# Seven products of sums of blocks for eight in the three last FFN stages of a float32 decoder trunk

## The chip, the core and the metric

The kernel runs on one core of a Trainium2 chip. The metric is the time on the device in microseconds, the median of several runs. TensorE is PE in the rows (its weight loads are PEld), VectorE is DVE, ScalarE is ACT, GpSimd is POOL, SyncE is SP. "us" is a microsecond.

## The reference

Two layers, each with two half-step SwiGLU FFNs around a mixer. The change is in the FFNs.

```python
D_MODEL = 1024; SEQ = 256; DEPTH = 2; D_FF = 2816
def _swiglu_ffn(h, w_in, w_out):
    gu = h @ w_in                      # (256, 1024) @ (1024, 5632)
    gate, up = jnp.split(gu, 2, axis=-1)
    return (jax.nn.silu(gate) * up) @ w_out

for i in range(DEPTH):
    x = x + 0.5 * _swiglu_ffn(_rmsnorm(x, ffn_norm[i, 0]), ffn_w_in[i, 0], ffn_w_out[i, 0])
    x = x + mixer(_rmsnorm(x, mix_norm[i]))     # layer 0: conv module, layer 1: differential attention
    x = x + 0.5 * _swiglu_ffn(_rmsnorm(x, ffn_norm[i, 1]), ffn_w_in[i, 1], ffn_w_out[i, 1])
```

## The kernel before

Six stages run one after the other: FFN, conv, FFN, FFN, attention, FFN, numbered 0 to 5. All weights come from HBM once, in units of 128 x 2048 float32 (1 MB), through three slots `raw`. Every matrix product is made of three in the round format fp32r: a weight `w` is split in `w_hi`, its rounding, and `w_lo`, the remainder, and so is the other side (`a_hi` and `a_lo` for the turned input of a stage, `h_hi` and `h_lo` for the turned hidden values). The product is the sum of hi x hi, hi x lo and lo x hi in PSUM (lines 563, 567 and 571). ACT does the roundings (`round_half`, line 985, 1024 columns each), DVE the remainders (`rest_half`, line 1397). Rounded forms stand in a ring of six places; ACT may overwrite a place once PE has begun the unit after the one that used it (`unit_begun`).

An FFN's 2816 hidden values go in 11 chunks of 256. A chunk has three units: two with its gate and up columns (one for each half of the 1024 inputs; `first_unit`, 24 matmuls of 512 columns each, over 4 blocks of inputs and 2 tiles of 128 tokens), and one with its rows of `w_out` (`second_unit`, 24 matmuls into `acc`, which holds the stage's sum in four banks). After the first two, ACT takes silu of the gate (line 1030) and DVE multiplies with up (`gated`, line 1489). The hidden values are turned by 16 DVE transposes of 32 partitions (`turn_hidden`, line 1497), rounded by ACT (`hidden`, line 1035), and DVE makes their remainder (line 1504). The second unit of a chunk stands one chunk later in PE's order, so all this has the time of the next chunk's first units. In PSUM a chunk takes the two banks of `pg`; the two of `pt` are for transposes.

The order on each engine is written by hand: `tick(n)` is the rounding or the remainder of unit n + 4, and the ticks stand between the steps of the chunks. At a stage's start (`enter`) DVE adds `acc` to `xs` (line 1413), multiplies with the norm's gain (1420), PE turns (667), ACT rounds (998), and squares are summed (1009).

## Time and profile before

| | |
|---|---|
| time, median of 3 runs | 951.86 us (951.72 to 951.97) |
| span of the profiled run | 950.0 us |
| PE busy, matmuls | 943.8 us, 4392 matmuls |
| DVE busy | 762.9 us |
| ACT busy | 495.2 us |
| from one FFN stage to the next (2 to 3) | 182.1 us |

The profile is one execution. Busy times of an engine are summed without overlap over its instructions; the mean of one matmul is longer than the distance to the next, since matmuls overlap. A releaser is what ended an engine's idle time.

### The profile page before, as it was taken

How to read it: one execution, taken by the hardware profiler on the slowest of the kernel's cores; microseconds unless marked ns; L12 is line 12 of the kernel's file. 1: busy time of each engine (PE TensorE's matmuls, PEld its weight loads, DVE VectorE, ACT ScalarE, POOL GpSimd, SP SyncE). 2: the span in 40 equal slices, each digit the busy share in tenths (PEclk: the TensorE clock that was granted, in tenths of full speed). 3: DMA queues.
4: the chain of work that ended last, by engine and by line, in shares of the span. 5: the costliest groups of instructions: out<-in, count | busy, mean ns of one | idle time of the engine just before them, and what ended most of it. 6: DMA issues, size and time to landing. Idle time of an engine off the chain costs nothing.

```text
span 950.0 us, 12305 instructions
## 1 busy us (share of the span) xinstructions
PE 943.8 (99%) x4392; PEld 778.6 (82%) x4392; DVE 762.9 (80%) x1447; ACT 495.2 (52%) x777; POOL 102.3 (11%) x94
## 2 busy tenths in 40 slices
PE   9999999999999999999999999999999999999998
PEld 7888888888978888888888888888778888888887
DVE  5778887879989887878788787877777888878782
ACT  6644353468755454444555344445778745444440
POOL 0100000068802000000000000001333100000000
PEclk9999999999999999999999999999999999999999
DMA  9876555544547636364554636353434545364521
GB/s 326 334 284 238 205 181 216 209 176 148 185 165 248 229 139 259 132 241 157 222 184 163 251 132 254 145 226 134 172 117 150 179 177 219 135 240 158 225 84 45
DMA packets 29548, 182.47 MB, mean 192 GB/s; under 512 B 3520, under 2 KB 3904, under 8 KB 9408
## 3 DMA queue, kind: packets, MB, share of 16 engines
q1 hardware_dynamic: 27360, 175.19, 48.9%
q0 software_dynamic: 2144, 6.70, 2.3%
q8 instruction: 26, 0.43, 0.2%
q14 instruction: 18, 0.15, 0.0%
HBM read 180.83 MB, written 1.05 MB: 191 GB/s over the span
## 4 chain that ended last, share of the span: by engine, by line
PE 98%; DMA 0%; DVE 0%; POOL 0%; ACT 0%; issue 0%; SPq 0%
PE pg L563 17%; PE pg L571 17%; PE pg L567 17%; PE acc L563 13%; PE acc L571 13%; PE acc L567 13%; PE pt L786 2%; PE pt L667 1%; PE acc L893 1%; PE pt L912 1%; DMA raw<-in_units 0%; PE acc L615 0%; PE pt L874 0%; PE acc L620 0%; PE acc L623 0%; PE pt L697 0%
## 5 line engine op out<-in xcount | busy, mean ns | idle before, releaser
L1397 DVE TENSOR_TENSOR w_lo<-raw,w_hi 128x1024 fp32r<-128x1024 f32 x304 | 356.4, 1221 | 18.2 <-ACT w_hi L985 16.9
L985 ACT CAST w_hi<-raw 128x1024 fp32r<-128x1024 f32 x314 | 311.2, 1046 | 20.7 <-DMA raw<-in_units 20.6
L563 PE MATMUL pg<-w_hi,a_hi 128*128 128x512 f32 x720 | 282.6, 392 | 0.0
L571 PE MATMUL pg<-w_hi,a_lo 128*128 128x512 f32 x720 | 280.3, 389 | 0.0
L567 PE MATMUL pg<-w_lo,a_hi 128*128 128x512 f32 x720 | 280.2, 389 | 0.0
L1497 DVE STREAM_TRANSPOSE mix<-hs 32x128 f32<-32x128 f32 x592 | 179.2, 303 | 8.9
L563 PEld LDWEIGHTS pg<-w_hi,a_hi 128*128 128x128 f32 x720 | 135.2, 188 | 28.7 <-issue 1.4
L571 PEld LDWEIGHTS pg<-w_hi,a_lo 128*128 128x128 f32 x720 | 135.2, 188 | 28.1
L567 PEld LDWEIGHTS pg<-w_lo,a_hi 128*128 128x128 f32 x720 | 135.3, 188 | 27.4
L1030 ACT ACTIVATE hs<-pg,rstd 128x256 f32<-128x256 f32 x80 | 37.8, 475 | 160.0 <-PE pg L571 160.0
L1489 DVE SCALAR_TENSOR_TENSOR hs<-pg,rstd,hs 128x256 f32<-128x256 f32 x80 | 38.2, 483 | 101.7 <-ACT hs L1030 101.7
L1035 ACT CAST h_hi<-mix 128x512 fp32r<-128x512 f32 x37 | 23.0, 622 | 174.6 <-DVE mix L1497 174.6
L563 PE MATMUL acc<-w_hi,h_hi 128*128 128x512 f32 x352 | 111.9, 392 | 0.0
L571 PE MATMUL acc<-w_hi,h_lo 128*128 128x512 f32 x352 | 111.1, 389 | 0.0
L567 PE MATMUL acc<-w_lo,h_hi 128*128 128x512 f32 x352 | 111.1, 389 | 0.0
L571 PEld LDWEIGHTS acc<-w_hi,h_lo 128*128 128x128 f32 x352 | 66.1, 188 | 13.9
L567 PEld LDWEIGHTS acc<-w_lo,h_hi 128*128 128x128 f32 x352 | 66.1, 188 | 13.7
L563 PEld LDWEIGHTS acc<-w_hi,h_hi 128*128 128x128 f32 x352 | 65.6, 188 | 13.4 <-DVE h_lo L1504 0.3
L563 PE MATMUL acc<-w_hi,a_hi 128*128 128x512 f32 x192 | 74.6, 409 | 0.0
L571 PE MATMUL acc<-w_hi,a_lo 128*128 128x512 f32 x192 | 71.3, 391 | 0.0
L567 PE MATMUL acc<-w_lo,a_hi 128*128 128x512 f32 x192 | 71.1, 391 | 0.0
L505 POOL TENSOR_TENSOR rstd<-msq,exponent 128x2 f32<-128x2 f32 x6 | 4.3, 709 | 432.4 <-DVE msq L1431 432.4
(161 smaller groups left out, 745.7 us busy)
## 6 DMA issues: line engine op xcount, KB each, us to landing
raw<-in_units SPq DMA_DIRECT2D x157, 1024.0 KB, 5.2
diags<-in_conv_diags SPq DMA_DIRECT2D x8, 512.0 KB, 4.2
raw<-in_units SPq DMA_DIRECT2D x12, 256.0 KB, 7.0
diags<-in_conv_diags POOLq DMA_DIRECT2D x4, 512.0 KB, 4.8
gain<-in_ffn_norm POOLq DMA_DIRECT2D x3, 512.0 KB, 4.8
xs<-in_x SPq DMA_DIRECT2D x4, 256.0 KB, 8.3
gain<-in_mix_norm POOLq DMA_DIRECT2D x2, 512.0 KB, 5.5
xg<-in_conv_b_in POOLq DMA_DIRECT2D x2, 512.0 KB, 4.1
```

The source lines that it names most:

```text
L563: mm = pe.matmul(dst[j], stat_hi, m_hi, start=first, stop=False)
L567: pe.matmul(dst[j], stat_hi, m_lo, start=False, stop=False)
L571: mm = pe.matmul(dst[j], stat_lo, m_hi, start=False, stop=last)
L667: mm = pe.transpose(pt[:, t, k * P:(k + 1) * P], xg[:, t, half * BANK + k * P:half * BANK + (k + 1) * P], ident)
L786: mm = pe.matmul(sums(VK + g // 2)[:, :, g % 2 * PC:(g % 2 + 1) * PC], up2[:, g, LAG - b:LAG - b + P], diags[:, h % DIAG_RING, i * P:(i + ...
L893: mm = pe.matmul(score_bank(TT * h + t, c), qT[d, h, t * P:(t + 1) * P], kT[d, h, 0:(t + 1) * P], start=True, stop=True)
L985: nc.scalar.copy(w_hi[n % RING][:, cols], raw[n % RAW][:, cols]).then_inc(hi_done, 1)
L1030: nc.scalar.activation(sil[:, t, :], src, ACT.Silu, scale=rstd[:, s, t:t + 1]).then_inc(silu_done, 1)
L1035: nc.scalar.copy(h_hi[:, c % 2, :, :].rearrange("p k n -> p (k n)"), pt[:, 0, :] if by_tensor(s, c) else hT.rearrange("p k n -> p (k n)")) ...
L1397: nc.vector.tensor_tensor(w_lo[n % RING][:, cols], raw[n % RAW][:, cols], w_hi[n % RING][:, cols].bitcast(F32), ALU.subtract).then_inc(lo_ ...
L1489: nc.vector.scalar_tensor_tensor(out=hid[:, t, :], in0=src, scalar=rstd[:, s, t:t + 1], in1=sil[:, t, :], op0=ALU.mult, op1=ALU.mult).then ...
L1497: mm = nc.vector.transpose(hT[b * 32:(b + 1) * 32, :, :].rearrange("p k (t n) -> p k t n", t=TT)[:, :, :, a * 32:(a + 1) * 32], hid[a * 32 ...
```

## The change

Stages 2, 3 and 5 (`FAST`) take chunk 0 as before and the ten others in five pairs. A pair has four blocks of `w_in`: b11 and b21 are its 512 gate columns for the first and the second half of the inputs, b12 and b22 its 512 up columns. Pairs 1 and 5 are plain: four units of 24 matmuls into `pg` and `pt`. Pairs 2, 3 and 4 have seven products of 12 matmuls: three with a block and four with a sum of blocks (u1 to u4), against blocks of x or sums of blocks of x, in Winograd's form of the scheme with seven products. The parts:

- DVE forms four sums of x a stage (`sum_x`), out of copies of the turned x that ACT makes at the stage's start (`keep`), and their hi and lo parts take one of the six places of the ring, so five are left.
- DVE forms u1 to u4 in place in the slots of the loads (`sum_weights`), four instructions of 128 x 2048 for a pair. There are six slots now: three lie in tiles that conv and attention use.
- A pair by blocks has nine forms (seven, and its two units of `w_out`) where a plain one has six. From a stage's fourth form on, roundings and remainders are one instruction of 2048 columns.
- Five DVE instructions combine the products of a pair, together with a copy that ACT makes of the first product (`keep_first`); three of the later products are added by PE onto values that still stand in PSUM.
- The hidden values of a pair are turned by one DVE transpose of 128 x 1024, which turns blocks of 32 x 32, and then 32 ACT copies of 32 partitions x 128 elements that put the blocks in place (`quadrants`, 16 for each chunk).
- The loops of stage 0 are written out, and the stages before a fast one prepare three forms in advance where it was four units.

```diff
+FAST = (2, 3, 5)
+MODES = ('plain', 'blocks', 'blocks', 'blocks', 'plain')
+ORDER = [("b11", "b21", "b12", "b22", "wa")] + [("b11", "u1", "wa", "u2", "b22", "u3", "b21", "u4", "wb") if mode == "blocks" else
+                                               ("b11", "b21", "wa", "b12", "b22", "wb") for mode in MODES[1:-1]] \
+    + [("b11", "b21", "b12", "b22", "wa", "wb", "wc", "wd")]
...
+            self.sums += [(s11, s12, l12), (s12, s22, l22), (s11, s22, l22), (s11, s21, l21)]
...
+                def by_sums_pair(d):
+                    g, q = pair_index(s, d), sums_before(s, d)
+
+                    pe.wait_ge(gates_done, 2 * g - 1)
+                    product(form_at(s, d, "b11"), x_block(0, 0), pg[:, 0, :], True)
...
+                    product(form_at(s, d, "u1"), mixed(2), pt[:, 0, :], True)
+                    seconds(2 * d - 3)
...
+                    product(form_at(s, d, "u2"), mixed(1), pt[:, 1, :], True)
+
+                    pe.wait_ge(combined_done, 5 * q + 1)
+                    product(form_at(s, d, "b22"), mixed(3), pt[:, 0, :], False)
+
+                    pe.wait_ge(combined_done, 5 * q + 2)
+                    product(form_at(s, d, "u3"), mixed(0), pt[:, 1, :], False)
+
+                    pe.wait_ge(kept_done, q + 1)
+                    product(form_at(s, d, "b21"), x_block(0, 1), pg[:, 0, :], False)
+
+                    pe.wait_ge(combined_done, 5 * q + 4)
+                    product(form_at(s, d, "u4"), x_block(1, 1), pt[:, 1, :], False)
+                    seconds(2 * d - 2)
...
+                def quadrants(g, k0, k1):
+
+                    act.wait_ge(blocks_turned, g + 1)
+                    for q in range(4):
+                        for b in range(4):
+                            src = gated_by[q * 32:(q + 1) * 32, b * 256:(b + 1) * 256]
+                            mm = nc.scalar.copy(
+                                hidden_turned[b * 32:(b + 1) * 32, k0:k1, :].rearrange("p k (t n) -> p t k n", t=TT)[:, :, :, q * 32:(q + 1) * 32],
+                                src.rearrange("p (t k n) -> p t k n", t=TT, k=4)[:, :, k0:k1, :])
+                    mm.then_inc(pair_turned, 1)
...
+                def by_sums_pair(d):
+                    g, b, n = pair_index(s, d), u + PAIR_AT[d], u + PAIR_AT[d + 1]
+                    round_form(b + 4)
+                    keep_first(d)
+                    hidden_pair(2 * d - 2, turned(d - 1, 2))
+                    for k in range(5, 9):
+                        round_form(b + k)
+                    round_form(n)
+                    round_form(n + 1)
+                    gates_of(d, 0)
+                    round_form(n + 2)
+                    round_form(n + 3)
+                    gates_of(d, 1)
+                    quadrants(g, 0, 2)
+                    hidden_pair(2 * d - 1, turned(d, 1))
+                    quadrants(g, 2, 4)
...
+                    nc.vector.tensor_tensor(places_raw[out], places_raw[out], places_raw[second], ALU.add).then_inc(weights_summed, 1)
...
+                def by_sums_pair(d):
+                    g, b, n = pair_index(s, d), u + PAIR_AT[d], u + PAIR_AT[d + 1]
+                    sum_weights(d, 3)
+                    rest_form(b + 4)
+                    hidden_pair(2 * d - 2)
+                    rest_form(b + 5)
+                    second_less(d)
+                    rest_form(b + 6)
+                    rest_form(b + 7)
+                    both_less(d)
+                    rest_form(b + 8)
+                    first_up(d)
+                    rest_form(n)
+                    last_up(d)
+                    first_sums(d + 1)
+                    rest_form(n + 1)
+                    third_sum(d + 1)
+                    gate_up(d, 0)
+                    rest_form(n + 2)
+                    last_gate(d)
+                    rest_form(n + 3)
+                    gate_up(d, 1)
+                    turn_blocks(g)
+                    hidden_pair(2 * d - 1)
```

The three functions `by_sums_pair` are PE's, ACT's and DVE's, in this order.

DVE before, in a chunk of stage 2: the product with the gates (L1489), the small transposes (L1497), the remainder of half a unit (L1397) and of the hidden values (L1504).

```order
L1489 SCALAR_TENSOR_TENSOR hs<-pg,rstd,hs 128x256 [waits silu_done] x2
L1497 STREAM_TRANSPOSE mix<-hs 32x4x32 [waits chunk_out]
L1497 STREAM_TRANSPOSE mix<-hs 32x4x32 x15
L1397 TENSOR_TENSOR w_lo<-raw,w_hi 128x1024 [waits hi_done]
L1504 TENSOR_TENSOR h_lo<-mix,h_hi 128x512 [waits h_hi_done]
L1397 TENSOR_TENSOR w_lo<-raw,w_hi 128x1024 [waits hi_done]
```

DVE of the change, around the end of pair 2's list and the start of pair 3's, in stage 2: remainders (L1842), a combination (L2008), a product with the gates (L2041), the wide transpose (L2048), the hidden remainder (L2054), the sum in place (L2000).

```order
L1842 TENSOR_TENSOR w_lo<-raw,w_hi 128x2048 [waits hi_done]
L2008 TENSOR_TENSOR xg<-pt,xg 128x512 [waits product_ready]
L1842 TENSOR_TENSOR w_lo<-mix,w_hi 128x2048 [waits hi_done]
L2041 SCALAR_TENSOR_TENSOR mix<-xg,rstd,mix 128x512 [waits combined_done,gates_done]
L2048 STREAM_TRANSPOSE mix<-mix 128x1024 [waits pair_gated]
L2054 TENSOR_TENSOR h_lo<-mix,h_hi 128x512 [waits h_hi_done]
L2000 TENSOR_TENSOR mix<-mix,diags 128x2048 [waits raw_ready4]
L1842 TENSOR_TENSOR w_lo<-diags,w_hi 128x2048 [waits hi_done]
```

The hidden remainder stood behind a unit's remainder, and stands right behind the transpose now; the sum and the next form's remainder are queued behind it.

ACT before, in a chunk of stage 2: the silu of a chunk (L1030), roundings of half a unit (L985) and the rounding of the hidden values (L1035).

```order
L1030 ACTIVATE hs<-pg,rstd 128x256 [waits chunk_done] x2
L985 CAST w_hi<-raw 128x1024 [waits unit_begun,raw_ready2]
L1035 CAST h_hi<-mix 128x512 [waits hid_turned]
L985 CAST w_hi<-raw 128x1024
```

ACT of the change, from the gates of pair 2 in stage 2 (L1451) on: copies into place (L1460), the hidden rounding (L1470), the form's rounding (L1312), the copy of the first product (L1438).

```order
L1451 ACTIVATE mix<-xg,rstd 128x512 [waits combined_done]
L1460 COPY mix<-mix 32x2x2x32 [waits blocks_turned]
L1460 COPY mix<-mix 32x2x2x32 x15
L1470 CAST h_hi<-mix 128x512 [waits unit_begun,pair_turned]
L1460 COPY mix<-mix 32x2x2x32 [waits blocks_turned]
L1460 COPY mix<-mix 32x2x2x32 x15
L1312 CAST w_hi<-raw 128x2048 [waits unit_begun,raw_ready2]
L1438 COPY xg<-pg 128x512 [waits mixed_lo_done,product_ready]
```

Between the silu and the hidden rounding stand 16 copies now, and 16 more between that and the next form's rounding.

## Rows read from the trace of the kernel before

**Rows 1.** The page's head, parts 1 and 2: busy us, share, instructions; granted clock in slices.
```profile
span 950.0 us, 12305 instructions
...
PE 943.8 (99%) x4392; PEld 778.6 (82%) x4392; DVE 762.9 (80%) x1447; ACT 495.2 (52%) x777; POOL 102.3 (11%) x94
...
PEclk9999999999999999999999999999999999999999
```

**Rows 2.** The waits of PE: who waited for whom, us in total, times, longest.
```profile
PE pg L672 <- DVE h_hi L1453: 1.4, 1, 1.4
PE acc L828 <- DVE xg L1651: 1.0, 2, 0.8
PE acc L615 <- ACT w_hi L1049: 0.6, 1, 0.6
```

**Rows 3.** Timeline of PE in stage 2: start, us busy, instruction, count.
```profile
342.78 0.39 PE L571 MATMUL pg<-w_hi,a_lo 128*128 128x512 f32 x1
...
344.82 0.39 PE L571 MATMUL pg<-w_hi,a_lo 128*128 128x512 f32 x1
```

**Rows 4.** Timeline of ACT: silu of chunk 0 in stages 2 and 3, and of two chunks between.
```profile
299.42 0.47 ACT L1030 ACTIVATE hs<-acc,rstd 128x256 f32<-128x256 f32 x1
...
344.57 0.47 ACT L1030 ACTIVATE hs<-pg,rstd 128x256 f32<-128x256 f32 x1 [4.16 <-PE pg L571]
...
360.89 0.47 ACT L1030 ACTIVATE hs<-pg,rstd 128x256 f32<-128x256 f32 x1 [4.15 <-PE pg L571]
...
481.52 0.47 ACT L1030 ACTIVATE hs<-acc,rstd 128x256 f32<-128x256 f32 x1
```

**Rows 5.** Windows: one chunk of stage 2; its length, then busy us of each engine.
```profile
328.70:345.02 16.32, 16.32 (x73) 13.52 (x72) 13.32 (x25) 7.25 (x10) 0.00 (x0) 1.00 0.52 200
```

**Rows 6.** Groups of DVE instructions in that chunk: count, busy us, mean ns, idle before.
```profile
L1397 DVE TENSOR_TENSOR w_lo<-raw,w_hi 128x1024 fp32r<-128x1024 f32 x6 | 7.0, 1220 | 0.0
L1497 DVE STREAM_TRANSPOSE mix<-hs 32x128 f32<-32x128 f32 x16 | 4.8, 303 | 0.2
L1489 DVE SCALAR_TENSOR_TENSOR hs<-pg,rstd,hs 128x256 f32<-128x256 f32 x2 | 1.0, 483 | 2.5 <-ACT hs L1030 2.5
L1504 DVE TENSOR_TENSOR h_lo<-mix,h_hi 128x512 fp32r<-128x512 f32 x1 | 0.7, 685 | 0.0
```

**Rows 7.** Timelines of ACT and DVE in stage 2: instructions in a row.
```profile
335.04 0.62 ACT L1035 CAST h_hi<-mix 128x512 fp32r<-128x512 f32 x1 [4.70 <-DVE mix L1497]
335.56 4.84 ACT L985 CAST w_hi<-raw 128x1024 fp32r<-128x1024 f32 x5
...
336.78 5.76 DVE L1397 TENSOR_TENSOR w_lo<-raw,w_hi 128x1024 fp32r<-128x1024 f32 x5
346.27 5.05 DVE L1497 STREAM_TRANSPOSE mix<-hs 32x128 f32<-32x128 f32 x16
```

**Rows 8.** Groups by form over the whole span: the same work at two widths.
```profile
L1397 DVE TENSOR_TENSOR w_lo<-raw,w_hi 128x1024 fp32r<-128x1024 f32 x304 | 356.4, 1221 | 18.2 <-ACT w_hi L985 16.9
L985 ACT CAST w_hi<-raw 128x1024 fp32r<-128x1024 f32 x314 | 311.2, 1046 | 20.7 <-DMA raw<-in_units 20.6
...
L1504 DVE TENSOR_TENSOR h_lo<-mix,h_hi 128x512 fp32r<-128x512 f32 x37 | 25.3, 684 | 0.0
...
L1035 ACT CAST h_hi<-mix 128x512 fp32r<-128x512 f32 x37 | 23.0, 622 | 174.6 <-DVE mix L1497 174.6
...
L1113 ACT COPY mix<-pt 64x128 f32<-64x128 f32 x12 | 3.1, 261 | 0.2
```

**Rows 9.** Timeline of DVE: instructions of 512 columns in a row.
```profile
236.43 1.40 DVE L1556 SCALAR_TENSOR_TENSOR mix<-acc,rstd,xg 128x512 f32<-128x512 f32 x2
...
468.34 0.69 DVE L1420 TENSOR_TENSOR xg<-xs,gain 128x512 f32<-128x512 f32 x1
468.95 0.68 DVE L1413 SCALAR_TENSOR_TENSOR xs<-acc,xs 128x512 f32<-128x512 f32 x1
```

**Rows 10.** Timeline of ACT: small copies and activations in a row.
```profile
241.11 2.18 ACT L1113 COPY mix<-pt 64x128 f32<-64x128 f32 x8
...
694.98 0.39 ACT L1226 ACTIVATE diags<-diags,mix 128x128 f32<-128x128 f32 x1
695.27 0.18 ACT L1226 ACTIVATION_READ_ACCUMULATOR diags<-diags,mix 128x1 f32 x1
```

**Rows 11.** Timelines of the entry of stage 3: PE, ACT and DVE.
```profile
471.70 0.47 PE L563 MATMUL acc<-w_hi,a_hi 128*128 128x512 f32 x1
...
473.50 1.03 ACT L985 CAST w_hi<-raw 128x1024 fp32r<-128x1024 f32 x1
...
475.21 0.60 PE L667 MATMUL pt<-ident,xg 128*128 128x128 f32 x4
476.33 0.60 PE L667 MATMUL pt<-ident,xg 128*128 128x128 f32 x4
...
479.01 0.17 DVE L1431 TENSOR_SCALAR msq<-msq 128x2 f32<-128x2 f32 x1
```

**Rows 12.** DMA issues: KB each, median us from issue to landing.
```profile
raw<-in_units SPq DMA_DIRECT2D x157, 1024.0 KB, 5.2
```

**Rows 13.** Timeline of PE at the very start: ten matmuls ahead of the first stage.
```profile
1.45 4.63 PE L672 MATMUL pg<-h_hi 128*128 128x512 f32 x10 [1.45 <-DVE h_hi L1453]
```

More of the change, by code:

```diff
@@ new lines, with by_sums @@
+assert MODES[0] == MODES[-1] == "plain"
+PAIR_AT = [None] + [2 + sum(len(forms) for forms in ORDER[:d]) for d in range(DOUBLES + 1)]
+FAST_FORMS = PAIR_AT[-1]
+SECOND_AT = [PAIR_AT[1 + d] + k for d in range(DOUBLES) for k, name in enumerate(ORDER[d]) if name[0] == "w"]
+def by_sums(d):
+    return MODES[d - 1] == "blocks"
+BEFORE = [None] + [sum(by_sums(e) for e in range(1, d)) for d in range(1, DOUBLES + 2)]
+READY = [None] + [sum(BLOCKS if by_sums(e) else 2 * TT for e in range(1, d)) for d in range(1, DOUBLES + 2)]
@@ L104 @@
+UNIT0, LOAD0 = PLAN.form0, PLAN.load0
+FORMS, LOADS = len(PLAN.forms), len(PLAN.loads)
 CONV, ATTN = 1, 4
@@ L720, in ffn @@
-                chunk(1, 0, True)
-                chunk(2, 0, False)
-                with pe.Fori(0, (FCH - 3) // 2 - 1) as i:
-                    chunk(3, i, False)
-                    chunk(4, i, False)
-                chunk(FCH - 2, 0, False)
-                chunk(FCH - 1, 0, False)
+                    first_unit(n, 0, banks)
+                    first_unit(n + 1, 1, banks, {4 if s == 0 else 3: lambda: turn_gated(0)} if first and by_tensor(s, 0) else {})
+                    hidden_ready(c - 1)
@@ L1019, in enter, with gate @@
                         square(s, half, t)
[L1020 removed]
+                    if s in FAST:
+                        for t in range(TT):
+                            keep(s, half, t)
+                    if s in FAST and half:
+                        round_form(n - 1)
+                    if s not in FAST:
+                        round_half(n, half)
             def ffn(s):
                 f, u, c0 = FFN0[s], UNIT0[s], CHUNK0[s]
[L1025 removed]
+                def gate(c):
                     for t in range(TT):
[L1028 removed]
+                        act.wait_ge(chunk_done, 2 * (c0 + c) + t + 1)
                         src = pg[:, t, 0:CH] if c else acc[:, 2 * t, 0:CH]
@@ L1096, in ffn @@
-                chunk(FCH - 2, 0, False)
-                chunk(FCH - 1, 0, False)
-                tick(u + 32)
+                tick(u)
+                hidden(0)
+                tick(u + 1)
+                gate(1)
+                tick(u + 2)
+                tick(u + 3, lambda: hidden(1))
+                tick(u + 4)
+                for c in range(2, FCH):
+                    n = u + 2 + 3 * (c - 1)
+                    tick(n)
+                    tick(n + 1)
+                    gate(c)
+                    tick(n + 2, lambda: hidden(c))
@@ L1188, in conv @@
                     silu(kt)
-                for w in range(1, 4):
+                for w in range(1, 3):
                     tick(u + 2 * chunks + w)
@@ L1526, in chunk @@
-                def chunk(c, i, skip_first):
+                tick(u)
+                hidden(0)
+                tick(u + 1)
+                gated(1)
+                tick(u + 2)
+                tick(u + 3, lambda: hidden(1))
+                tick(u + 4)
+                for c in range(2, FCH):
                     n = u + 2 + 3 * (c - 1)
-                    if not skip_first:
-                        tick(n, i)
-                    tick(n + 1, i)
-                    gated(c, i)
+                    tick(n)
+                    tick(n + 1)
+                    gated(c)
@@ L1871, in pairs, with wide @@
         return w.reshape(-1, 2, P, D).transpose(0, 2, 1, 3).reshape(-1, P, UNIT)
-    out = np.empty((UNITS, P, UNIT), np.float32)
+    def wide(w):
+        w = w.reshape(2, 4, P, 2, F)[..., CH:].reshape(2, 4, P, 2, DOUBLES, BANK)
+        return w.transpose(4, 3, 0, 2, 1, 5).reshape(DOUBLES, 2, 2, P, UNIT)[:, ::-1]
+    out = np.empty((LOADS, P, UNIT), np.float32)
     for s, (kind, layer, which, chunks) in enumerate(STAGES):
-        u = UNIT0[s]
-        if kind == "ffn":
+        u = LOAD0[s]
+        if s in FAST:
+            first, second = halves(ffn_w_in[layer, which]), pairs(ffn_w_out[layer, which])
+            out[u:u + 2] = first[0]
+            blocks = wide(ffn_w_in[layer, which])
+            u, p = u + 2, 0
+            block_of = {"b12": 0, "b22": 1, "b11": 2, "b21": 3}
+            for d in range(DOUBLES):
+                order = ("b11", "b12", "b22", "wa", "b21", "wb") if by_sums(d + 1) else ORDER[d]
+                for name in order:
+                    if name in block_of:
+                        out[u] = blocks[d].reshape(4, P, UNIT)[block_of[name]]
+                    else:
+                        out[u] = second[p]
+                        p += 1
+                    u += 1
+        elif kind == "ffn":
             first, second = halves(ffn_w_in[layer, which]), pairs(ffn_w_out[layer, which])
```

624 lines of the change are left out of this document (503 added, 121 removed).

## The prediction

> **What bounds the kernel now.** I read the page's head first: PE is busy for 943.8 of 950.0 us, DVE for 80% and ACT for 52%, and the granted clock is at its upper level, 2.4 GHz, in all 40 slices [rows 1]. The list of PE's waits has three entries, the longest 1.4 us [rows 2]. So TensorE's issue of matmuls is the time. Their pace is not the 389 ns that one is busy, since they overlap: from the start at 342.78 to that at 344.82 are nine steps, 0.2267 us each [rows 3]. A chunk of 72 matmuls is then 16.32 us, and the gate of one chunk stands 16.32 us behind that of the one before, 344.57 and 360.89 [rows 4].
>
> The second reading is how near the others are. In those 16.32 us DVE is busy for 13.32 us [rows 5]: six remainders of half units, 16 small transposes, two products with the gates, one hidden remainder [rows 6]. It has 3 us to spare for a chunk, 6 for a pair. A change that shortens PE and lengthens DVE must be summed on both.
>
> **What goes from PE.** A pair by blocks has 7 products of 12 matmuls where it had 8: 84 + 48 = 132 for 144, and 132 x 0.2267 = 29.9 us for 32.6. Nine such pairs (three in each of three stages) lose 108 matmuls, 24.5 us. That is all that can be won on PE.
>
> **The price of a wide instruction.** No instruction of 2048 columns stands in the trace. DVE's remainders of 1024 columns follow each other every (5.76 - 1.22) / 4 = 1.135 us [rows 7], and 512 more columns cost 1221 - 684 = 537 ns [rows 8]. So 2048 columns are 1.135 + 1.07 = 2.21 us; two half ones, 2.27, are the upper end, and the lower is the 1.22 of one half, if width were free, for which no row speaks. The sums in place read and write f32 as these do and get the same price. On ACT (4.84 - 1.04) / 4 = 0.95 us, plus 1024 columns at (1046 - 622) / 512 ns, is 1.80 us [rows 7, 8]. Instructions of 512 columns are 0.60 us on DVE (one begins at 468.34, the next at 468.95) [rows 9] and 0.52 on ACT (335.04 to 335.56) [rows 7]; a product with the gate out of PSUM is 1.40 for two less 0.74 for the second, 0.66 [rows 9].
>
> **DVE's list for a pair by blocks.** Nine forms have a remainder each, since every form, sum or not, is split in two parts; four sums come on top. 13 x 2.21 = 28.7 us. Five combinations of products: 3.0. Two products with the gates: 1.3. One transpose of 128x1024 in place of 32 small ones: between 303 ns plus 896 columns at 1.05 ns = 1.25 and eight times 0.303 = 2.4; I take 1.27, because the cost by column of every other DVE instruction is 1.05 ns. Two hidden remainders: 1.2. Together 35.5 us, against 29.9 on PE and 32.6 now. **DVE alone is already longer than the pair of before**, although 10 us of small transposes are gone: three more remainders and four sums are 15.5 us.
>
> **What DVE waits for in it.** Behind the wide transpose the next DVE instruction is the remainder of hidden chunk 2d-1. It waits for ACT's 16 copies of 32 partitions and the rounding of 512 columns, and all that is queued on DVE waits behind it: the last sum and the remainder of b22. Eight copies of 64x128 out of PSUM, the last 0.26 long, step by (2.18 - 0.26) / 7 = 0.27 us; an activation of 128x128 from SBUF to SBUF is followed 0.29 us later [rows 8, 10]. I take 0.28, so 4.5 for 16, plus 0.52 and 0.3 for three handovers: 5.3 us idle. Then ACT does 16 more copies, 4.5, and rounds b22, 1.8: 6.3, of which DVE covers 0.6 + 2.2. That is 3.5 idle. 35.5 + 5.3 + 3.5 = **44.3 us for a pair by blocks, in a circle that PE does not set**. PE has work for 29.9 of them. It stands some 8.5 us before the second product of hidden chunk 2d-1, 3 us before b22 (second_less behind a remainder), 2.3 before u3 (both_less).
>
> The Trainium skill, "VectorE: DVE Perf Modes", section on the TRN2 errata, speaks against the copies: ScalarE from SBUF to SBUF costs a fixed 224 cycles beside one per column at 1.2 GHz, so many small tiles pay it each time. By it a copy of 128 columns would be an estimated 0.293 us and the sum below some 6 us more; the trace's 0.27 and 0.29 agree.
>
> **A stage, from its first matmul.** Before, stage to stage is 481.52 - 299.42 = 182.1 us [rows 4]. DVE is done with the stage's entry at 479.2 for a first matmul at 471.70, so at 7.5 [rows 11]; ACT's four new copies of the turned x and one wide rounding let the remainder of the fourth form end at 12.2. Up to hidden chunk 1 the list holds seven remainders 15.5, three sums 6.6, two gated 1.0, 16 transposes 5.05 [rows 7], nine short ones with the sums of x 5.7, gates 1.3, transpose 1.3, waits of 0.9, then 5.3 + 0.6: 12.2 + 43.2 = 55.4. Here PE loses first: its own work would let it begin that second product at 44.6. Pairs 2 and 3 add 44.3 each, pair 4 lacks the three sums for a next pair, 37.6: hidden chunk 7 is ready at 181.6. PE is through with pair 4 some 7.5 us earlier, at 174.1: behind last_up DVE still has three remainders, five shorter instructions and the wait, 15.7 us, and PE only the last product and one second unit, 8.2. The plain pair 5 is eight units of 24 matmuls, 43.5, with a wait of 1.4 for hidden chunk 10 behind 32 copies: 219.0. The difference is 36.9 us for a stage. The copies of x at the entry are hidden: the first two begin on ACT where a rounding began at 473.50, so end at 474.6, and the transposes that wait for them began at 475.21 and 476.33 [rows 11]; if that cover fails it costs a microsecond. DMA isn't in it: 1 MB lands in 5.2 us [rows 12], six loads for a pair have 44 us, and the slot of a pair's b12, freed by the remainder of b22, has over 10 us until the first sum wants its data. The loops written out in stage 0 I cost at nothing; within half a microsecond either way.
>
> Sum: 950.0 + 3 x 36.9 = 1060.7 us of span; the median stands 1.9 over the span of the profiled run, so **1062.6 us**, 11.6% more.
>
> **Rivals.** (a) *PE's count decides*: 951.9 - 24.5 = 927.4 us, faster. It needs DVE's list and its waits within 29.9 us: with 13 wide instructions it would hold only if one took under 1.2 us and the copies were nearly free. The row of 1024 columns at 1.22 speaks against it. 0.03. (b) *The copies don't hold DVE up*, being far shorter with 32 partitions than the rows say: with copies at nothing the waits shrink to 0.7 and the circle to 36.2, hidden chunk 7 is ready at 51.0 + 36.2 + 36.2 + 29.6 = 153.0, pair 5 begins at 150.2, the stage is 193.7 and the time 951.9 + 3 x 11.6 = 987 us. Nothing in rows 10 shows a copy below 0.26. 0.05. (c) *The clock falls in PE's waits*. Nothing in this trace has PE wait over 1.4 us behind its start, and the clock stays up. If it fell in the waits of 8.5 us and came back soon, the lost time would lie in the 13 us that PE stands anyway. If it stayed at 1.2 GHz in the pairs by blocks, their matmuls would go at the pace of the ten at the very start, (4.63 - 0.64) / 9 = 0.443 us [rows 13], so 58.5 us for a pair, 14.2 more, nine times: 1190 us. 0.06.
>
> The Trainium skill, "TensorE: Matmul & The Clock Gate", Part 1, has this rule: an idle array drops to half its clock and activity brings it back. The trace has no such wait to test it on.
>
> **How the numbers follow.** The forecast, a circle of DVE and ACT, 0.85; (b) 0.05, (c) 0.06, (a) 0.03, anything else 0.01. Within the forecast: copies of 0.20 us would give 1036 (stage 210.0), of 0.31 1077; a transpose of 2.4 adds 18; remainders of 2.27 add 9; handovers may be twice as long, 3 more. The range from 1022 to 1110 takes these in and leaves out (a), (b) and (c), 0.14, with a little of the forecast's own tails. A difference of 0.2% is about what a measurement of this kernel can tell from none. Faster has (a) and a little for an overlap that I don't see, 0.04; same 0.01; slower 0.95.
>
> **What would show it.** DVE's wide remainders and sums at 2.2 to 2.3 us, 117 and 36 of them; 15 transposes near 1.3; the copies of 32 partitions at 0.27 to 0.3 each; the gate of one pair by blocks 44 us behind the last; DVE's idle time before the hidden remainder released by ACT's rounding, near 5 us each; PE waiting some 8 us for h_lo and 2 to 3 us each for combinations; granted clock below 1 behind the long waits without effect. PE's busy share would be near 87%. I am wrong if wide instructions cost less than 1.5 us, if ACT's copies run while DVE has other work, or if PE shows waits for its own slow products.

## The result, and the profile after

The changed kernel takes 1078.96 us (median of 4 runs, 1077.7 to 1081.0), the kernel before, on the same chip, 951.79. The ratio is 1.134, with a 95% interval from 1.132 to 1.136. The forecast was 1062.6 in a range from 1022 to 1110. The profiled execution has a span of 1079.2 us; it is the slowest of the four (1081.0 us). Of its page, the head and the rows of busy tenths (40 slices of 27 us):

```profile
span 1079.2 us, 11805 instructions
PE 960.7 (89%) x4272; PEld 777.8 (72%) x4272; DVE 817.4 (76%) x1042; ACT 688.8 (64%) x1197; POOL 101.7 (9%) x94
PE   9999999999996868699977686998999996867798
DVE  5778787798887969656796786757778786968753
ACT  6644444586465674877548567686878556674884
PEclk9999999999998989899998898999999998989899
...
PE 47%; DVE 28%; ACT 14%; issue 8%; DMA 3%; SPq 0%; POOL 0%; DVEq 0%; ACTq 0%; POOLq 0%
```

In [rows 1] PE was busy in 99% of the span and the clock row was full. Now PE drops to 6 to 8 tenths in the three stages that were changed, the clock row has gaps in the same places, and the chain that ended last (its shares by engine are the last line) runs through DVE and ACT for 42% of the span. Yet neither DVE nor ACT is busy much more than three quarters of the time: what bounds these stages is an order of steps, not one full engine. The waits (engine, its line and who released it; us in total, times, longest) say which order:

```profile
DVE h_lo L2054 <- ACT h_hi L1470: 99.0, 19, 5.6
PE acc L774 <- DVE h_lo L2054: 61.5, 11, 8.8
DVE w_lo L1842 <- ACT w_hi L1312: 49.8, 20, 3.9
```

Line 2054 is the remainder of a hidden, 1470 its rounding on ACT, behind the small copies of line 1460, 774 PE's first product in a unit, 2048 the wide transpose, 1842 and 1312 the remainder and the rounding of a 2048-column form. PE's longest wait was 1.4 us in [rows 2] and is 8.8 now. Here is DVE from one wide transpose to the next, pair 3 of stage 2 (start, duration, line; in brackets the idle time before it and its releaser):

```profile
384.82 1.25 DVE L2048 STREAM_TRANSPOSE mix<-mix 128x1024 f32<-128x1024 f32 x1
391.68 0.69 DVE L2054 TENSOR_TENSOR h_lo<-mix,h_hi 128x512 fp32r<-128x512 f32 x1 [5.61 <-ACT h_hi L1470]
392.29 2.28 DVE L2000 TENSOR_TENSOR diags<-diags,raw 128x2048 f32<-128x2048 f32 x1
398.42 2.29 DVE L1842 TENSOR_TENSOR w_lo<-raw,w_hi 128x2048 fp32r<-128x2048 f32 x1 [3.84 <-ACT w_hi L1312]
...
429.89 1.25 DVE L2048 STREAM_TRANSPOSE mix<-mix 128x1024 f32<-128x1024 f32 x1
436.75 0.69 DVE L2054 TENSOR_TENSOR h_lo<-mix,h_hi 128x512 fp32r<-128x512 f32 x1 [5.61 <-ACT h_hi L1470]
```

One turn, 391.68 to 436.75, is 45.07 us. Two waits are in it, 3.84 and the 5.61 before 436.75; the other 35.62 us are DVE's instructions without a gap. ACT behind the first of the two transposes:

```profile
386.10 4.89 ACT L1460 COPY mix<-mix 32x128 f32<-32x128 f32 x16 [3.42 <-DVE mix L2048]
391.03 0.62 ACT L1470 CAST h_hi<-mix 128x512 fp32r<-128x512 f32 x1
391.55 4.90 ACT L1460 COPY mix<-mix 32x128 f32<-32x128 f32 x16
396.48 1.91 ACT L1312 CAST w_hi<-raw 128x2048 fp32r<-128x2048 f32 x1
```

The first 16 copies fill the wait of 5.61 us before the hidden, the second 16 and the rounding behind them most of the 3.84.

### The profile page after: what moved, and what is told of

Its sections match the earlier page's. It is cut to its first block, busy times and chain, and to the rows that moved or that the text cites. A ratio compares the mean times of both kernels' runs of the same rounds, so it can differ in the third digit from the quotient of the medians.

```text
span 1079.2 us, 11805 instructions
## 1 busy us (share of the span) xinstructions
PE 960.7 (89%) x4272; PEld 777.8 (72%) x4272; DVE 817.4 (76%) x1042; ACT 688.8 (64%) x1197; POOL 101.7 (9%) x94
## 4 chain that ended last, share of the span: by engine, by line
PE 47%; DVE 28%; ACT 14%; issue 8%; DMA 3%; SPq 0%; POOL 0%; DVEq 0%; ACTq 0%; POOLq 0%
DVE w_lo L1842 13%; ACT mix L1460 9%; PE acc L774 7%; PE acc L782 6%; PE acc L778 6%; PE pg L774 5%; PE pg L782 5%; PE pg L778 5%; ACT w_hi L1312 3%; DMA raw<-in_units 3%; DVE raw L2000 2%; PE pt L1097 2%; DVE diags L2000 2%; DVE w_lo L1832 1%; DVE mix L2041 1%
## 5 line engine op out<-in xcount | busy, mean ns | idle before, releaser
L1460 ACT COPY mix<-mix 32x128 f32<-32x128 f32 x480 | 142.0, 296 | 62.4 <-DVE mix L2048 57.2
L1832 DVE TENSOR_TENSOR w_lo<-raw,w_hi 128x1024 fp32r<-128x1024 f32 x124 | 146.5, 1223 | 23.9 <-ACT w_hi L1303 23.6
L1303 ACT CAST w_hi<-raw 128x1024 fp32r<-128x1024 f32 x134 | 134.1, 1047 | 16.7 <-DMA raw<-in_units 16.5
L774 PE MATMUL pg<-w_hi,a_hi 128*128 128x512 f32 x336 | 133.2, 396 | 0.1
L782 PE MATMUL pg<-w_hi,a_lo 128*128 128x512 f32 x336 | 130.9, 390 | 0.0
L778 PE MATMUL pg<-w_lo,a_hi 128*128 128x512 f32 x336 | 130.8, 389 | 0.0
L1842 DVE TENSOR_TENSOR w_lo<-raw,w_hi 128x2048 fp32r<-128x2048 f32 x51 | 116.4, 2287 | 14.0 <-ACT w_hi L1312 13.5
L1842 DVE TENSOR_TENSOR w_lo<-diags,w_hi 128x2048 fp32r<-128x2048 f32 x42 | 95.9, 2286 | 34.0 <-ACT w_hi L1312 34.0
L1312 ACT CAST w_hi<-raw 128x2048 fp32r<-128x2048 f32 x51 | 96.9, 1908 | 31.9 <-DVE raw L2000 22.3
L1312 ACT CAST w_hi<-diags 128x2048 fp32r<-128x2048 f32 x42 | 80.1, 1912 | 38.8 <-DVE diags L2000 22.8
L2054 DVE TENSOR_TENSOR h_lo<-mix,h_hi 128x512 fp32r<-128x512 f32 x30 | 20.7, 690 | 99.0 <-ACT h_hi L1470 99.0
L782 PEld LDWEIGHTS acc<-w_hi,h_lo 128*128 128x128 f32 x352 | 69.0, 196 | 15.2
L774 PEld LDWEIGHTS pg<-w_hi,a_hi 128*128 128x128 f32 x336 | 63.1, 188 | 13.9 <-issue 1.6
```

Of the source, the lines that this page charges most:

```text
L774: mm = pe.matmul(dst[j], stat_hi, m_hi, start=first, stop=False)
L778: pe.matmul(dst[j], stat_hi, m_lo, start=False, stop=False)
L782: mm = pe.matmul(dst[j], stat_lo, m_hi, start=False, stop=last)
L1303: nc.scalar.copy(hi_of(n)[:, cols], raw_of(n)[:, cols]).then_inc(hi_done, 1)
L1312: nc.scalar.copy(hi_of(n)[:, :], raw_of(n)).then_inc(hi_done, 1)
L1460: mm = nc.scalar.copy(hidden_turned[b * 32:(b + 1) * 32, k0:k1, :].rearrange("p k (t n) -> p t k n", t=TT)[:, :, :, q * 32:(q + 1) * 32], ...
```

## The experiments

Ratios are to the kernel before on the same chip. Differences from the change and between experiments go across chips, on which the kernel before had medians from 951.7 to 952.0 us. Where three lines of a difference say the edit, the rest is left out. "A turn" is, as above, the time from the remainder of hidden chunk 3 to that of chunk 5, in the profiled execution of the run, in stage 2.

**1. Without the seven products.**

```diff
-MODES = ('plain', 'blocks', 'blocks', 'blocks', 'plain')
+MODES = ('plain', 'plain', 'plain', 'plain', 'plain')
```

> All five pairs of chunks are computed without sums of blocks; the chunks stay joined by pairs, with the wide transpose and the 32 small copies on ScalarE, so only the seven-product part is taken back. Circle theory (in a pair by blocks VectorE's list of 35.5 us and the first 16 copies of 4.9 us run one after the other): a plain pair has 12 wide instructions fewer on VectorE's path (6 remainders against 9, no sums, no combinations), its list is some 16 us, and TensorE is the bound again with 144 matmuls x 0.2267 = 32.6 us a pair; 952 to 962 us. If the pairing itself, the wide transpose or the copies cost as such, whatever VectorE's list holds: 1030 us or more, up to 1079. If the clock of TensorE in the product waits were the cost: also about 952, but then no reading of VectorE's list would be needed; the other runs tell that apart.

Measured: 954.31 us, ratio 1.0025 (1.0015 to 1.0035). The pairing, the wide transpose and the copies stay in it and cost 2.3 us in all, though DVE waits for copies as before (396.97 below). Such a wait costs next to nothing while PE has a list of 32.6 us for a pair and DVE's own work is some 18 (the turn less its waits). The twelve instructions that the expectation counts are seven of 2048 columns and five combinations of 512.

```profile
396.97 0.69 DVE L2054 TENSOR_TENSOR h_lo<-mix,h_hi 128x512 fp32r<-128x512 f32 x1 [3.23 <-ACT h_hi L1470]
429.60 0.69 DVE L2054 TENSOR_TENSOR h_lo<-mix,h_hi 128x512 fp32r<-128x512 f32 x1 [3.22 <-ACT h_hi L1470]
```

429.60 - 396.97 = 32.63 us: the pair is PE's 144 matmuls.

**2. One pair by blocks in a stage.**

```diff
-MODES = ('plain', 'blocks', 'blocks', 'blocks', 'plain')
+MODES = ('plain', 'blocks', 'plain', 'plain', 'plain')
```

> Of the three pairs by blocks of a stage only pair 2 is left; pairs 3 and 4 are computed plain. Circle theory: the loss is 45.1 us against 32.6 for each turn of the circle from one hidden (2d-1) to the next, so that one pair costs about a third of the 127 us, and a little more, since the way into and out of a pair by blocks is paid once whatever their number: 995 to 1005 us (951.8 + 3 x 14 to 17). If several pairs by blocks in a row cost more than in proportion (the three make each other late), one pair alone would cost 960 to 975 us.

Measured: 1000.04 us. That is 48.0 us over the kernel before, and 45.7 us over the all-plain pairs for three such pairs, where nine cost 124.7. It is near proportion (15.2 each against 13.9).

**3 to 5. Copies and sums taken away, one by one and together.**

```diff
-                    for q in range(4):
-                        for b in range(4):
+                    for q in range(1):
+                        for b in range(1):
...
-nc.vector.tensor_tensor(places_raw[out], places_raw[out], places_raw[second], ALU.add)
+nc.vector.tensor_tensor(spare[:, m:m + 1], places_raw[out][:, 0:1], places_raw[second][:, 0:1], ALU.add)
```

The first half alone:

> Two of the 32 small copies of a pair are left, one for each chunk (the rest of the turned hidden is left out, so the output is not the reference's). Circle theory: each group of 16 copies stands in the circle between the transpose and the remainder of the hidden (2d-1), and the second group before the rounding of hidden (2d-2); taking 15 x 0.306 = 4.6 us out of each hold of the list, and both groups off ScalarE's road to the next pair's roundings: 45.1 us becomes about 36, three stages with three pairs by blocks: 1079 - 83 = 990 to 1000 us. If the copies run beside VectorE's work (rival b of the prediction): 1075 to 1080 us. If the clock of TensorE or its waits for the products decide: 1075 to 1080 us too.

Measured: 995.61 us. The turn is 414.58 - 377.56 = 37.0 us:

```profile
414.58 0.69 DVE L2054 TENSOR_TENSOR h_lo<-mix,h_hi 128x512 fp32r<-128x512 f32 x1 [1.01 <-ACT h_hi L1470]
```

The second half alone:

> The 36 sums of blocks of weights are left out on VectorE (each is replaced by the addition of one column into a place of its own; the forms are then rounded from the plain blocks, so the output is not the reference's). Circle theory: four instructions of 2.285 us leave VectorE's list in each pair, but one of them (the fourth, ahead of the remainder of b22) stood in an idle time that the copies make, so 4 x 2.2 = 8.8 us at most, and by working the lists through about 4.4 us a pair, as ScalarE and the copies then hold: 1079 - 40 = 1039 us (1030 to 1050). If VectorE's list held alone, 9 x 8.8 = 79 us: 1000 us. If VectorE's list is not the bound: 1075 to 1080 us.

Measured: 1040.14 us, with a turn of 40.7. Four sums are 8.8 us of DVE's list, but 4.4 come back: 2.1 as idle time where the fourth sum had stood between the hidden and the remainder of b22 (5.98 us for 3.84, below), 1.9 in a wait for a rounding at 408.11, and 0.3 for the four additions of one column:

```profile
383.02 0.69 DVE L2055 TENSOR_TENSOR h_lo<-mix,h_hi 128x512 fp32r<-128x512 f32 x1 [5.62 <-ACT h_hi L1471]
383.63 0.15 DVE L2001 TENSOR_TENSOR spare<-diags,raw 128x1 f32<-128x1 f32 x1
389.76 2.29 DVE L1843 TENSOR_TENSOR w_lo<-raw,w_hi 128x2048 fp32r<-128x2048 f32 x1 [5.98 <-ACT w_hi L1313]
```

Both:

> The changes of the runs with one copy for a chunk and without the sums of blocks, together (the output is not the reference's). Circle theory: the circle shrinks below TensorE's 29.9 us for a pair, so TensorE is the bound again and the 24.5 us of matmuls that the change removed begin to show: 943 to 955 us, that is at or a little below the kernel before. If something else than VectorE's list and the copies holds the pair (waits between the products, the clock): 990 us or more.

Measured: 946.09 us, ratio 0.994 (0.992 to 0.995). These three settle the cause: without the copies the time falls by 83 us, without the sums by 39, and without both by 133 us, below the kernel before. Even then a turn is 31.3 us where 132 matmuls are 29.9; PE still waits 0.62 and 0.81 us in one (at 337.47 and 349.48). So what the seven products gave here with their sums and nearly all of their turning left out is 6 us (0.6%), and not the 24.5 us (2.6%) of the count.

**6. The turning back on DVE.** Two calls of 16 transposes of 32x32 blocks for each pair, as in the kernel before, in place of the wide one; the copies are dropped.

```diff
-                    nc.vector.transpose(gated_by.rearrange("p (a m n) -> p a m n", a=4, m=8),
-                                        wide.rearrange("p t (k a n) -> p a (t k) n", a=4, n=32)).then_inc(blocks_turned, 1)
+                    for k in range(0, 4, 2):
+                        for a in range(4):
+                            for b in range(4):
+                                mm = nc.vector.transpose(
...
+                        mm.then_inc(pair_turned, 1)
```

> The hidden is turned as in the kernel before: 32 transposes of 32x32 blocks on VectorE a pair (16 for each chunk) in place of one wide transpose and 32 copies on ScalarE. Circle theory: VectorE's list grows by 32 x about 0.31 - 1.25 = 8.8 us a pair, and the 16 copies of 4.9 us that stood in the circle, with the wait for them, go, and ScalarE has 9.8 us less to do. Nearly even: 1076 to 1086 us, a little slower. If the copies on ScalarE are what costs as such: 1079 - 83 = about 1000 us. If VectorE's list holds and the copies stand beside it: 1079 + 15 x 8.8 = 1150 us or more.

Measured: 1078.78 us, the same as the change. The two ways are even:

```profile
428.53 10.12 DVE L2045 STREAM_TRANSPOSE mix<-mix 32x128 f32<-32x128 f32 x32
438.68 0.69 DVE L2053 TENSOR_TENSOR h_lo<-mix,h_hi 128x512 fp32r<-128x512 f32 x1
```

DVE has no idle time before the hidden now, but 10.12 us of transposes where it had 1.25 and 9.45 of waiting. A turn is 44.6 us. DVE is busy for 88% of the span instead of 76%, which alone would have looked like a worse kernel.

**7. More work for PE.**

```diff
+                    if by_sums(d - 1):
+                        pe.wait_ge(combined_done, 5 * q)
+                    else:
+                        pe.wait_ge(pair_gated, 2 * g)
+                    for _ in range(30):
+                        pe.matmul(pt[:, 1, :], a_hi[:, 0, 0:P], a_hi[:, 0:2, :].rearrange("p k n -> p (k n)"), start=True, stop=True)
                     seconds(2 * d - 3)
```

> In each of the nine pairs by blocks TensorE gets 30 matmuls more, of 512 columns, into a bank that is free, in its wait of 8.8 us before the second matmul of chunk 2d-3: 270 matmuls, 61 us at 0.2267 us. Circle theory: TensorE has room there (8.8 us against 6.8), so the time stays at 1079 us within 3 us; the granted clock no longer falls in that place, which may give back up to 2 us in a stage in the last of its pairs by blocks (the wait of 1.26 us of VectorE at 461 us), so 1073 to 1081. If TensorE's count of matmuls decides: 1079 + 61 = 1140 us. If the lower clock behind the waits is what costs (about 13 matmuls at 0.43 us in each pair, 2.6 us x 9): 1055 us.

Measured: 1079.56 us; 61 us more of matmuls are free. In pair 3 of stage 2 the clock now stays at its upper level in that place (1.00 from 391 to 400 us), and the turn is as long as before (45.10 us):

```profile
384.01 6.96 PE L997 MATMUL pt<-a_hi 128*128 128x512 f32 x30
393.02 0.73 PE L774 MATMUL acc<-w_hi,h_hi 128*128 128x512 f32 x2 [2.05 <-DVE h_lo L2060]
...
438.12 0.73 PE L774 MATMUL acc<-w_hi,h_hi 128*128 128x512 f32 x2 [2.03 <-DVE h_lo L2060]
```

In pair 4 it falls all the same (0.50 from 440 to 442 us), as it does in pair 3 behind a longer wait before b22, 3.31 us at 404.79 (0.50 from 406 to 408). So the run shows PE's room, and not what a clock that never falls would give. The 24.5 us that the change took from PE were worth nothing for the same reason.

**8 and 9. Two mends that compute everything.** First the order: on ACT the roundings, and on DVE the last sum and the remainders of two forms of the next pair, go ahead of the copies and of the hidden.

```diff
+                def ahead(d):
+                    if by_sums(d + 1):
+                        sum_weights(d + 1, 3)
+                        rest_form(u + PAIR_AT[d + 1] + 4)
+                        rest_form(u + PAIR_AT[d + 1] + 5)
...
                     turn_blocks(g)
+                    ahead(d)
                     hidden_pair(2 * d - 1)
```

> Nothing is computed otherwise; on ScalarE the roundings of the next pair's forms u3 and of l22 (n + 4 and n + 5) are moved ahead of the first 16 copies, and on VectorE the fourth sum of blocks and both remainders ahead of the remainder of hidden (2d-1), wherever the next pair goes by blocks. Circle theory: VectorE now works through its idle time of 5.6 us before the hidden's remainder, and the circle is left with what is then the longer of VectorE's list and ScalarE's road: about 40 us, 1079 - 42 = 1037 us (1028 to 1050). If the number of instructions and not their order decides, or the ring of forms (five places) keeps the roundings back: 1075 to 1080 us.

Measured: 1052.57 us, a gain of 26 where some 42 were expected. The wait before hidden (2d-1) is gone as foreseen (390.01), and another stands before hidden (2d-2), which now has nothing in front of it that covers the second 16 copies. Behind it come two smaller waits for roundings:

```profile
390.01 0.68 DVE L2060 TENSOR_TENSOR h_lo<-mix,h_hi 128x512 fp32r<-128x512 f32 x1
395.28 0.69 DVE L2060 TENSOR_TENSOR h_lo<-mix,h_hi 128x512 fp32r<-128x512 f32 x1 [4.58 <-ACT h_hi L1470]
...
397.09 2.29 DVE L1848 TENSOR_TENSOR w_lo<-raw,w_hi 128x2048 fp32r<-128x2048 f32 x1 [0.52 <-ACT w_hi L1312]
400.60 2.29 DVE L1848 TENSOR_TENSOR w_lo<-diags,w_hi 128x2048 fp32r<-128x2048 f32 x1 [1.21 <-ACT w_hi L1312]
```

The turn is 42.0 us. Then the copies, 16 of 32x256 instead of 32 of 32x128:

```diff
-                                hidden_turned[b * 32:(b + 1) * 32, k0:k1, :].rearrange("p k (t n) -> p t k n", t=TT)[:, :, :, q * 32:(q + 1) * 32],
-                                src.rearrange("p (t k n) -> p t k n", t=TT, k=4)[:, :, k0:k1, :])
+                                hidden_turned[b * 32:(b + 1) * 32, :, :].rearrange("p k (t n) -> p t k n", t=TT)[:, :, :, q * 32:(q + 1) * 32],
+                                src.rearrange("p (t k n) -> p t k n", t=TT, k=4))
```

> 16 copies of 32x256 for both chunks of a pair in place of 32 copies of 32x128, all ahead of the rounding of hidden (2d-1). The time of such a copy is not known here; by the row of the 512-column rounding (0.52 us for 512 columns) and that of 128 columns (0.306 us a step) it lies between 0.31 and 0.41 us. Circle theory: the second group of copies goes from ScalarE's road to the next pair's first rounding, the first group gets longer by 16 x (0 to 0.1) us; 1045 to 1065 us. If only the first group's length mattered (the wait of VectorE before the hidden's remainder): 1079 to 1094 us.

Measured: 1053.94 us. A copy of 256 columns takes 0.413 us a step (6.60 us for 16), against 0.306 for 128 columns.

```profile
385.05 6.60 ACT L1462 COPY mix<-mix 32x256 f32<-32x256 f32 x16 [3.42 <-DVE mix L2050]
392.34 0.69 DVE L2056 TENSOR_TENSOR h_lo<-mix,h_hi 128x512 fp32r<-128x512 f32 x1 [7.32 <-ACT h_hi L1472]
```

Only 1.2 us of its gain is in this turn (43.86). Pair 4's turn is 3.8 us shorter, and the plain pair behind it, from hidden chunk 7 to the stage's end, 4.2: there the second 16 copies had held the chunk 8 up.

**10 to 12. Both mends, and the extra matmuls with them.** The edits are those above (in runs 10 and 11 one form goes ahead and not two, that of b22, the form n + 4, which the expectation calls u3's); run 12 is the earlier forms with the 30 matmuls.

> Both mends together: 16 joined copies of 0.413 us (6.61 us, as the run with the joined copies showed), and on ScalarE the rounding of u3's form (n + 4), on VectorE the fourth sum and that form's remainder ahead of the hidden's remainder. Circle theory: VectorE's idle time before the hidden shrinks from 7.3 to some 3 us and no second group of copies is waited for, so the circle is about 40 us in place of 45.1, 1036 us if the clock costs nothing and up to 1050 if TensorE's slower matmuls behind its wait of some 8 us stand in the circle as in the run with the earlier forms. If the two mends take away the same idle time and not two: 1050 to 1055 us.

Measured: 1051.87 us. The idle time before the hidden is 2.95 us as expected, and the turn is 43.5 all the same. What is late next:

```profile
391.02 0.69 DVE L2061 TENSOR_TENSOR h_lo<-mix,h_hi 128x512 fp32r<-128x512 f32 x1 [2.95 <-ACT h_hi L1472]
391.76 1.22 PE L774 MATMUL acc<-w_hi,h_hi 128*128 128x512 f32 x2 [10.52 <-DVE h_lo L2061]
399.88 0.39 PE L957 MATMUL pt<-w_hi 128*128 128x512 f32 x1
400.36 1.91 ACT L1312 CAST w_hi<-diags 128x2048 fp32r<-128x2048 f32 x1 [4.77 <-PE pt L957]
402.30 2.29 DVE L1849 TENSOR_TENSOR w_lo<-diags,w_hi 128x2048 fp32r<-128x2048 f32 x1 [3.39 <-ACT w_hi L1312]
```

This is one chain through three engines: the hidden lets PE begin its 24 matmuls, the start of the next product (399.88) frees a place in the ring of forms, ACT rounds into it, DVE takes the remainder. The 24 matmuls last 399.88 - 391.76 = 8.12 us; at 0.2267 us they would be 5.4. The windows of that stretch (us, busy time of PE, PEld, DVE, ACT and POOL, then the granted clock) have the reason:

```profile
392.00:396.00 4.00, 4.00 (x10) 3.13 (x11) 2.88 (x2) 3.58 (x2) 0.00 (x0) 0.50 0.04 10
396.00:400.00 4.00, 4.00 (x16) 3.24 (x16) 2.91 (x3) 0.00 (x0) 0.00 (x0) 0.84 0.67 229
```

Behind PE's wait of 10.5 us the granted clock is at 0.50, the level of 1.2 GHz, and here, other than in the change itself, it stands in the turn: 2.7 us of 43.5. The two runs that should have shown it by keeping the clock up mostly didn't do so.

> As the run before, with the 30 extra matmuls in each pair by blocks. With the clock up in TensorE's wait the circle is VectorE's list (35.5 us) and what is left of its wait for the copies (some 3 us, and the wait for the forms): 1030 to 1038 us, the best of the versions with all their sums. If the clock plays no part: the same time as without the extra matmuls, within 3 us.

Measured: 1049.99 us (1047.9 to 1054.7), the same within 3 us and not the 1030 to 1038 of a clock kept up; turn 43.9. The 30 matmuls are over before the wait is: PE then stands another 3.77 us, and the two matmuls behind it take 1.22 us, the lower level. One turn is different. In stage 3, behind a wait as long, the clock stays up, and the turn of pair 4 is 34.42 us, where those of stages 2 and 5, at the lower level, are 35.89 and 36.79:

```profile
647.83 0.73 PE L774 MATMUL acc<-w_hi,h_hi 128*128 128x512 f32 x2 [3.76 <-DVE h_lo L2067]
```

> The order of the run with the earlier forms (1052.6 us against an expected 1037), with the 30 matmuls more of the run with the extra matmuls in TensorE's wait. In the run with the earlier forms TensorE waits 9.66 us for the hidden, takes 7.4 us for its 24 matmuls at the lower clock where 5.45 are usual, and then runs product after product, while ScalarE waits for the ring's places and VectorE for ScalarE (0.5 and 1.4 us): there the clock stands in the circle. If so, keeping the clock up gives back 1.5 to 2 us in each of nine pairs: 1035 to 1041 us. If the clock has no part in it: 1050 to 1055. If TensorE's count decides: 1100 and more.

Measured: 1052.31 us, where 1035 to 1041 were expected. Here PE stands 2.90 us after the extra matmuls and the clock falls within the next microsecond (0.72 in 390 to 392 us, 0.50 in the two after). The 24 matmuls take 397.32 - 390.12 = 7.2 us instead of 7.4, and the turn is 41.8 instead of 42.0. In pair 2 the 30 matmuls are themselves in the way: they are still running when the hidden is ready, and PE's product begins 3.6 us behind the start of its remainder instead of 0.7 (turn 42.86 for 42.84).

How much the clock costs in the mended versions can be read from the turns of all three stages, since its level behind the wait differs from one to the next. Of the turns of pairs 2 and 3 (us; "24 matmuls" is from the first matmul of the product behind the wait to the first of u2 on `pt`):

| version | 24 matmuls | turn | turn less the 24 matmuls |
|---|---|---|---|
| the change | 6.94 to 7.46 | 45.07 to 45.09 | 37.6 to 38.2 |
| earlier forms (8) | 7.08 to 8.36 | 41.64 to 42.92 | 34.56 in all six |
| joined copies (9) | 7.54 to 8.47 | 42.95 to 43.86 | 35.39 to 35.41 |
| both (10) | 6.90 to 8.27 | 42.30 to 43.67 | 35.39 to 35.41 |

In the change the turn takes no notice of these matmuls. In every mended version it follows them one for one: there PE stands in the circle, and what the lower clock adds to the 5.44 us of 24 matmuls goes into the turn. The turn of pair 4 in runs 10 and 11 says the same down to 5.59 us (34.42 less 5.59 is 28.83, and so is 35.75 less 6.92). Over the nine turns of run 10 the 24 matmuls take 68.2 us where they would take 49.0 at the upper level, so an estimated 19 us of its 1051.9 are the clock; the wait of 3.39 us behind them is long enough for that. Without them it would be at some 1033, near the 1036 expected of it with the clock at no cost. In run 8 the wait behind these matmuls is shorter (1.21 us where they take 7.42), so below 6.2 us they would no longer count; that leaves an estimated 13 us, and 1040 for the 1037 expected. No run shows these two times. None of the mended versions comes near the kernel before, which remains the fastest that computes everything.

## Why the prediction was right, and where it was off

- **A wide instruction, 2.21 and 1.80 us.** Right. In DVE's timeline they follow each other every 2.20 us (414.64, 416.84, 419.04), ACT's every 1.81 (399.28, 401.10, 402.91). They are busy 2.29 and 1.91 us. DVE's remainders, the wide transposes and ACT's copies by groups (count, then busy us and mean ns):

```profile
L1842 DVE TENSOR_TENSOR w_lo<-raw,w_hi 128x2048 fp32r<-128x2048 f32 x51 | 116.4, 2287 | 14.0 <-ACT w_hi L1312 13.5
L2048 DVE STREAM_TRANSPOSE mix<-mix 128x1024 f32<-128x1024 f32 x15 | 18.7, 1245 | 0.5
L1460 ACT COPY mix<-mix 32x128 f32<-32x128 f32 x480 | 142.0, 296 | 62.4 <-DVE mix L2048 57.2
```

- **DVE's list, 35.5 us.** Right: 35.62. The wide transpose was the term with the widest bounds (1.25 to 2.4); it took 1.245, the price by column.
- **The two waits, 5.3 and 3.5.** Right in place, 0.65 us too short together (5.61 and 3.84). The mis-sized term is the copy: 0.28 was taken, between the neighbours 0.27 and 0.29 of [rows 8, 10], and 16 copies take 4.90 us, 0.306 each. The prediction's own bound for copies of 0.31 us gave 1077 us. The Trainium skill's estimate from "VectorE: DVE Perf Modes", errata for TRN2, 0.293 us, is the duration of one copy here (0.296) and was nearer than the rows from which I took my value.
- **The turn, 44.3.** 45.07. PE doesn't set it, as experiment 7 shows from the other side.
- **Pair 4, 37.6.** 40.1 (436.75 to 476.83). 0.65 are the copies; 1.3 are a wait that the sum did not have; the last 0.5 are gaps of 0.2 us and less and the list's own 0.1. PE stood 1.99 us before u3 (forecast 2.3; before b22 it was 1.8 for 3), and its matmuls went slowly behind that, so ACT got a place in the ring late:

```profile
454.26 0.69 PE L957 MATMUL pt<-w_hi 128*128 128x512 f32 x1 [1.99 <-DVE xg L2018]
459.18 1.91 ACT L1312 CAST w_hi<-diags 128x2048 fp32r<-128x2048 f32 x1 [2.24 <-PE pg L957]
461.12 2.29 DVE L1842 TENSOR_TENSOR w_lo<-diags,w_hi 128x2048 fp32r<-128x2048 f32 x1 [1.26 <-ACT w_hi L1312]
```

  Pair 4 has no sums for a next pair that would cover this. The prediction let the clock fall "without effect"; that held in pairs 2 and 3, and not in pair 4. Stage 5 is the counter-case: there the clock stayed up behind a wait as long, DVE did not wait for the rounding, and the same turn took 38.49 us (40.08 in stages 2 and 3). In experiment 7 it is pair 4 of stage 3 that keeps the clock, with 38.50 us against 40.11 and 40.07. So the clock costs 1.6 us in such a pair.

```profile
1018.45 0.50 PE L957 MATMUL pt<-w_hi 128*128 128x512 f32 x1 [1.97 <-DVE xg L2018]
```
- **A stage, +36.9 three times.** This is the step that failed most. The forecast's median, 1062.6, lacks 16.4 us of the measured 1078.96. Its span, 1060.7, lacks 18.5 of the 1079.2 of the profiled execution, which is 2 us over the median; 16.4 of these 18.5 are here, and 1.9 at the start. From PE's turns of the next stage's x:

```profile
289.20 0.60 PE L880 MATMUL pt<-ident,xg 128*128 128x128 f32 x4
...
514.39 0.60 PE L880 MATMUL pt<-ident,xg 128*128 128x128 f32 x4
...
741.19 0.66 PE L880 MATMUL pt<-ident,xg 128*128 128x128 f32 x4 [1.48 <-DVE xg L1865]
```

  Stages 2 and 3 take 225.2 and 226.8 us where the same turns stood 182.0 and 182.1 apart: 43.2 and 44.7 more. The difference between them is the wait of 1.48 us at 741.19. Stage 5 (to the span's end) has 39.2 more, 4.0 less than stage 2: 1.6 are its pair 4, and 2.3 the wait for hidden chunk 10, which it doesn't have, since no forms of a next stage stand before that chunk's remainder on DVE. Of the 6.3 us that stage 2 has over the forecast, two turns are 1.5, pair 4 is 2.5, the way from the stage's first matmul (291.44) to the end of hidden chunk 1's remainder is 0.5 (55.9 for 55.4), and the wait for hidden chunk 10 is 2.33 us (before PE's matmul at 510.16) instead of 1.4, 0.9. The last 0.9 I can't place.

- **The start, taken as unchanged.** It is 1.9 us longer (289.20 against 287.32). That need not be the code of stage 0: over the kernels here with the same first two stages, PE's first turn of stage 1 begins anywhere from 187.78 (one pair) to 190.47 us (joined copies), and in the kernel before at 187.85.
- **Rival (a)**, PE's count: fell with the result, and with experiment 7. **Rival (b)**, copies that don't hold DVE: experiment 3 is nearly its case (one copy of each 16 is left), and its 987 us came out as 995.6, which is nearer than the forecast was, since the term of the copies is left out of it. **Rival (c)**, the clock staying at 1.2 GHz: it falls behind PE's waits and comes back while PE works. The change's windows show 0.50 from 388 to 396 us, around PE's restart at 392.43, and 0.95 from 396 to 400; the mean over the span is 0.95. At the lower level a matmul steps by 0.427 us, where the prediction took 0.443. The direction is the one that the Trainium skill has ("TensorE: Matmul & The Clock Gate", Part 1), and these rows agree.

## What to carry to other kernels

Fewer products by sums of blocks trade matmuls for full-width passes of the vector engine; count those passes against the room that it has in a pair (here 6 us) before counting matmuls. Where a step goes from one engine to another and back, everything that is queued behind the return waits with it: sum the list plus the waits, and compare that circle with the engine that was the bound. When such a wait is mended, look for the next one first, since here mends of 26 and 25 us, joined with one form ahead for two, gave 27. Look also at whether the engine that waited has come into the circle: its slower clock cost the change 1.6 us in two of its nine pairs and nothing in the others, and an estimated 19 us in the version with both mends.
